# A fused transformer kernel: the chosen experts' rows gathered token by token, against both expert tables read once in blocks and multiplied densely

## What is computed

```python
q = (hf @ wq).reshape(T, 8, 2, 128)
sc = einsum('thpd,pnd->thpn', q, subkeys)          # 2 x 128 scores for each head
top_v, top_i = top_k(sc, 16)
cand_v = top_v[:, :, 0, :, None] + top_v[:, :, 1, None, :]
cand_id = top_i[:, :, 0, :, None] * 128 + top_i[:, :, 1, None, :]
best_v, best_j = top_k(cand_v.reshape(T, 8, -1), 16)
ids = take_along_axis(cand_id, best_j); gates = softmax(best_v)
a = einsum('td,ted->te', x, take(u_tab, ids))      # 128 chosen experts for each token
w = gates * gelu(a)
y = einsum('te,ted->td', w, take(v_tab, ids))
```

## Time and profile before

| | |
|---|---|
| time, median of 3 runs | 1234.37 us (1232.9 to 1235.4) |
| profiled execution, first to last instruction | 1229.3 us |
| mean granted clock of TensorE | 0.907 of full speed |
| busy: TensorE products / VectorE / ScalarE / GpSimd | 82% / 52% / 22% / 43% of the span |
| read from HBM | 360.08 MB, 294 GB/s over the span |

### The profile page before, as it was taken

How to read it: one execution, slowest core, us unless ns; L and a number is a source line. 1 busy time by engine, 2 the same in 40 slices (tenths; PEclk the granted TensorE clock), 3 DMA queues, 4 the chain that set the end, 5 groups by cost and what they waited for, 6 DMA issues and landing times.

```text
span 1229.3 us, 11227 instructions
## 1 busy us (share of the span) xinstructions
PE 1009.4 (82%) x3303; PEld 544.6 (44%) x3303; DVE 638.0 (52%) x1482; ACT 274.1 (22%) x741; POOL 534.5 (43%) x589
## 2 busy tenths in 40 slices
PE   4999999799888519767867857777579999999998
PEld 4768557554443204323323323323224645566454
DVE  6447676684754339636737646664443324311532
ACT  4022322112211102111105111110111253313540
POOL 1300003566666757667657667575766001200100
PEclk9999999899989859979779868887778999999999
DMA  9997765899999989989999989898989736333300
GB/s 346 308 371 253 277 212 163 318 366 336 356 365 362 413 340 357 373 334 400 347 353 398 350 347 408 325 413 335 412 342 364 269 137 206 95 111 137 137 1 34
DMA packets 123697, 361.75 MB, mean 294 GB/s; under 512 B 13464, under 2 KB 20256, under 8 KB 123520
## 3 DMA queue, kind: packets, MB, share of 16 engines
q0 software_dynamic: 76000, 276.39, 59.3%
q1 hardware_dynamic: 45008, 82.97, 19.1%
q10 hardware_dynamic: 2640, 1.81, 0.5%
HBM read 360.08 MB, written 1.05 MB: 294 GB/s over the span
## 4 chain that ended last, share of the span: by engine, by line
PE 74%; issue 14%; DVE 5%; another core or an unknown queue 3%; DMA 2%; ACT 2%; POOL 0%; DVEq 0%; POOLq 0%; ACTq 0%
PE bank L1492 36%; PE bank L1536 13%; PE bank L1256 9%; PE bank L1305 2%; PE bank L1246 2%; PE bank L1237 2%; DVE R L1784 1%; PE bank L1574 1%; PE bank L1346 1%; DMA small<-in_c 1%; PE bank L1322 1%; PE bank L1438 1%; PE bank L1417 1%; PE bank L1269 1%
## 5 line engine op out<-in xcount | busy, mean ns | idle before, releaser
L1492 PE MATMUL bank<-wring,R 128*128 128x512 f32 x496 | 238.9, 628 | 54.6 <-issue 53.0
L2040 DVE CUSTOM_DVE_ANT_0 wring<-wring,bank 128x1024 f32<-128x1024 f32 x160 | 194.2, 1218 | 150.2 <-DMA wring<-in_peer_u,ids 108.7
L769 POOL DMA_INDIRECT wring<-in_peer_v,ids x160 | 152.2, 951 | 125.4 <-issue 61.2
L1492 PEld LDWEIGHTS bank<-wring,R 128*128 128x128 f32 x496 | 98.2, 200 | 191.4 <-issue 186.8
L769 POOL DMA_INDIRECT wring<-in_peer_u,ids x160 | 152.9, 956 | 52.0 <-issue 44.2
L1536 PE MATMUL bank<-wring,hT 128*128 128x512 f32 (+1 forms) x384 | 167.4, 588 | 3.0 <-ACT R L1187 2.5
L1492 PE MATMUL bank<-R,modb 128*128 128x512 f32 x192 | 93.8, 635 | 58.3 <-ACT modb L998 38.2
L808 POOL TENSOR_SCALAR small<-small 128x2 f32<-128x2 f32 (+3 forms) x16 | 3.1, 194 | 304.4 <-ACTq L865 160.7
L1536 PEld LDWEIGHTS bank<-wring,hT 128*128 128x128 f32 x384 | 71.1, 190 | 83.8 <-issue 79.6
L1492 PE MATMUL bank<-hT,modb 128*128 128x512 f32 x96 | 63.2, 758 | 50.9 <-issue 49.1
L1492 PEld LDWEIGHTS bank<-R,modb 128*128 128x128 f32 x192 | 38.7, 203 | 111.6 <-issue 72.6
(11 more groups left out here) (292 smaller groups left out, 1326.4 us busy)
## 6 DMA issues: line engine op xcount, KB each, us to landing
wring<-in_w_in SPq DMA_DIRECT2D x12, 2048.0 KB, 12.1
wring<-in_ada_w SPq DMA_DIRECT2D x8, 2048.0 KB, 13.5
wring<-in_w_out SPq DMA_DIRECT2D x6, 2048.0 KB, 10.4
wring<-in_ada_w SPq DMA_DIRECT2D x8, 1024.0 KB, 14.7
wring<-in_peer_wq SPq DMA_DIRECT2D x2, 2048.0 KB, 7.9
wring<-in_w_in SPq DMA_DIRECT2D x4, 1024.0 KB, 10.6
wring<-in_w_in SPq DMA_DIRECT2D x2, 1792.0 KB, 12.6
wring<-in_peer_u,ids POOLq DMA_INDIRECT x160
```

Source lines behind the costliest of these rows:

```text
L769: pool.indirect_dma_start(dst, None, table, bass.IndirectOffsetOnAxis(index, 0)).then_inc(landed, 16)
L1492: last = pe.matmul(pb[half][:, :], diag[b][:, s, :], v_place(n, b, s)[:, half * 512:(half + 1) * 512], start=False, stop=closing and s == ...
L2040: dve.tensor_tensor_reduce(row, row, h_psum(t), 1.0, 0.0, ALU.mult, ALU.add, a8[:, b, s:s + 1]).then_inc(u_free, 1)
```

## The change

The gathers go away. SP reads U in 128 blocks of 128 experts (0.5 MB each, in order), TensorE transposes each block (8 transposes) and multiplies it with all 256 tokens (8 products of 256 columns), and ScalarE stores the Gelu of all 16384 x 256 activations in `experts`, which covers `wring` and `R` together. VectorE chooses for all heads in one go, and softmax is taken once. Then each token gets a dense 128x128 map of its gates: VectorE writes for every token two one-hot matrices of 128x128 (`left` and `right`, one of them scaled by the gates; `sides`), TensorE multiplies them (`gate_maps`, four tokens in a bank), and VectorE multiplies the map into `experts` for the blocks that are done (`j` of them), while ScalarE copies the rest of the map to where later blocks will stand; such a later block is parked and multiplied in when it is there. At last V is read in 128 blocks and multiplied densely, in both tiles for 112 blocks, then 16 blocks for tile 0 and the same 16 backwards for tile 1 (10 of them are read again). The queries and the scores stand in TensorE's sequence before and between the first blocks. Core of the diff:

```diff
+BLOCKS = 128
+GATES_FROM = 48
+U_PLACES = 3
+PARKED = 5
+V_PLACES = 6
+TAIL = 16
+TOKENS = 4
+BATCHES = NT * P // TOKENS
+def expert_schedule():
+    router = [("pq", 0, 0), ("pq", 0, 1), ("T", 0), ("sc", 0, 0), ("sc", 1, 0)]
+    rest = []
+    for ch in range(1, 4):
+        rest += [("pq", ch, 0), ("pq", ch, 1), ("sc", 0, ch), ("sc", 1, ch)]
+    out = list(router)
+    for j in range(BLOCKS):
+        if j + 1 < BLOCKS:
+            out.append(("T", j + 1))
+        out.append(("act", j))
+        if j < len(rest):
+            out.append(rest[j])
+        if j == GATES_FROM - 6:
+            out.append(("exp",))
+        if j == GATES_FROM - 3:
+            out += [("sel", t) for t in range(NT)]
+        done = sum(job[0] == "G" for job in out)
+        if j >= GATES_FROM:
+            out += [("G", b) for b in range(done, min(done + 1 + j % 2, BATCHES))]
+    return out
...
+def value_uses():
+    both = [(j, t, j) for j in range(BLOCKS - TAIL) for t in range(NT)]
+    first = [(j, 0, j) for j in range(BLOCKS - TAIL, BLOCKS)]
+    second = [(BLOCKS - 1 - m, 1, BLOCKS - 1 - m if m < V_PLACES else BLOCKS + m - V_PLACES) for m in range(TAIL)]
+    return both + first + second
...
+        experts = store[:, :].rearrange("p (j t) -> p j t", t=S)
+        u_rows = [modb[:, i, :] for i in range(U_PLACES)]
+        uT = [hrow[:, i, :].rearrange("p (k n) -> p k n", k=KD) for i in range(2)]
...
             await_full(sp, ("ada", 11))
             sp.wait_ge(rows_ready, 4 * NT)
-            sp.dma_start(fourth_queries, chunk_dram(peer_wq, 0, 1536, 2048)).then_inc(queries_landed[3], 16)
+            for j in range(BLOCKS):
+                if j >= U_PLACES:
+                    await_full(sp, ("T", j - U_PLACES, 1))
+                sp.dma_start(u_rows[j % U_PLACES], peer_u[0, j * P:(j + 1) * P, :]).then_inc(u_landed[j % U_PLACES], 16)
...
-            sp.wait_ge(u_free, NG * GROUP)
+            for n, (j, place) in enumerate(value_loads()):
+                if n == 0:
+                    await_full(sp, ("G", BATCHES - 1))
+                elif n == 2:
+                    await_full(sp, ("T", BLOCKS - 1, 1))
+                elif n == 5:
+                    sp.wait_ge(merged, len(merge_of))
+                elif n >= V_PLACES:
+                    sp.wait_ge(v_free, n - V_PLACES + 1)
+                sp.dma_start(v_rows[place], peer_v[0, j * P:(j + 1) * P, :]).then_inc(v_landed[place], 16)
...
+                elif job[0] == "T":
+                    j = job[1]
+                    if j >= 2:
+                        await_full(act, ("act", j - 2))
+                    for g in range(2):
+                        pb = await_full(act, ("T", j, g))
+                        free(act.activation(uT[j % 2][:, 4 * g:4 * g + 4, :], quad(pb[:, :]), ACT.Copy), ("T", j, g))
+                elif job[0] == "act":
...
+                elif job[0] == "exp":
+                    act.wait_ge(softmax_shift, 1)
+                    act.activation(chosen[:, :, 2, :], chosen[:, :, 2, :], ACT.Exp).then_inc(gate_exp, 1)
...
+            def transpose_experts(j):
+                pe.wait_ge(u_landed[j % U_PLACES], 16 * (j // U_PLACES + 1))
+                for g in range(2):
+                    pb = claim(pe, ("T", j, g))
+                    for i in range(4):
+                        a = (4 * g + i) * P
+                        last = pe.transpose(pb[:, i * P:(i + 1) * P], u_rows[j % U_PLACES][:, a:a + P], ident)
+                    full(last, ("T", j, g))
+
+            def activations(j):
+                for g in range(2):
+                    drained(pe, ("T", j, g))
+                pb = claim(pe, ("act", j))
+                for k in range(KD):
+                    last = pe.matmul(pb[:, 0:S], uT[j % 2][:, k, :], hT[:, k, :], start=k == 0, stop=k == KD - 1)
+                full(last, ("act", j))
+            def gate_maps(b):
+                pe.wait_ge(sides_ready, b + 1)
+                pb = claim(pe, ("G", b))
+                for i in range(TOKENS):
+                    last = pe.matmul(pb[:, i * P:(i + 1) * P], left[b % 2][:, i, :], right[b % 2][:, i, :], start=True, stop=True)
+                full(last, ("G", b))
...
+            for n, (j, t, load) in enumerate(uses):
+                place = loads[load][1]
...
                 for half in range(2):
+                    last = pe.matmul(pb[:, :], experts[:, j, t * P:(t + 1) * P], v_rows[place][:, half * 512:(half + 1) * 512], start=first, stop=final)
...
+            transpose_tile("zT", 0, 4 * NT, 0)
...
+            def sides(b):
+                for i in range(TOKENS):
+                    dve.tensor_scalar(left[b % 2][:, i, :], iota, chosenT[:, t, 0, c + i:c + i + 1], None, ALU.is_equal)
+                for i in range(TOKENS):
+                    ins = dve.tensor_scalar(right[b % 2][:, i, :], iota, chosenT[:, t, 1, c + i:c + i + 1],
+                                            chosenT[:, t, 2, c + i:c + i + 1], ALU.is_equal, ALU.mult)
+                ins.then_inc(sides_ready, 1)
+            for job in expert_schedule():
+                if job[0] == "G":
...
+                    w = experts[:, 0:j, b * TOKENS:(b + 1) * TOKENS]
+                    free(dve.tensor_tensor(w, quad(pb[:, :]).rearrange("p t n -> p n t")[:, 0:j, :], w, ALU.mult), job)
+                    if b + 2 < BATCHES:
+                        sides(b + 2)
```

More of the change, by code:

```diff
@@ L184, in y_schedule, with before, value_loads @@
     return out
[L187 to L195, removed]
+def expert_schedule():
[18 more added lines that the diff above has]
+    return out
+def before(job, kind):
+    order = expert_schedule()
+    return sum(e[0] == kind for e in order[:order.index(job)])
+def value_uses():
[3 more added lines that the diff above has]
+    return both + first + second
+def value_loads():
+    loads = [(j, j % V_PLACES) for j in range(BLOCKS)]
+    loads += [(BLOCKS - 1 - V_PLACES - m, (BLOCKS - 1 - m) % V_PLACES) for m in range(TAIL - V_PLACES)]
+    return loads
 def mla_schedule():
@@ L437, in program @@
[L437 to L458, removed]
@@ L968, in _ @@
             evac_oT(1)
[L969 to L974, removed]
             for t in range(NT):
@@ new lines, in transpose_choice @@
+            def transpose_choice(t):
+                if t == 0:
+                    pe.wait_ge(chosen_ready, 1)
+                pb = claim(pe, ("sel", t))
+                for i in range(3):
+                    last = pe.transpose(pb[:, i * P:(i + 1) * P], chosen[:, t, i, :], ident)
+                full(last, ("sel", t))
+            def gate_maps(b):
[4 more added lines that the diff above has]
+                full(last, ("G", b))
@@ new lines, in _ @@
+            drained(pe, ("G", BATCHES - 1))
+            loads = value_loads()
+            uses = value_uses()
+            for n, (j, t, load) in enumerate(uses):
+                place = loads[load][1]
+                if all(u[2] != load for u in uses[:n]):
+                    pe.wait_ge(v_landed[place], 16 * sum(e[1] == place for e in loads[:load + 1]))
+                if t == 0 and j in merge_of:
+                    pe.wait_ge(merged, merge_of[j] + 1)
+                first = all(u[1] != t for u in uses[:n])
+                final = all(u[1] != t for u in uses[n + 1:])
+                for half in range(2):
+                    pb = claim(pe, ("peer", t, half)) if first else bank[banks.jobs[("peer", t, half)][0]]
+                    last = pe.matmul(pb[:, :], experts[:, j, t * P:(t + 1) * P], v_rows[place][:, half * 512:(half + 1) * 512], start=first, stop=final)
+                    if final:
+                        full(last, ("peer", t, half))
+                if not final and all(u[2] != load for u in uses[n + 1:]):
+                    last.then_inc(v_free, 1)
@@ L1903, in _, with add_gated @@
             scale_heads(1)
-            def add_gated(job, gate, ch, t, ready=None):
+            def add_gated(job, gate, ch, t, ready=None, ytmp=ytmp):
                 pb = await_full(dve, job)
@@ new lines, in _, with choose @@
+            pairs = [(cand[:, h, :], best_v[:, h, :], best_j[:, h, :]) for h in range(2)]
+            def choose(t, g):
+                drained(dve, ("sc", t, g))
+                k, here = 4 * t + g, slice(g * 2 * TOPK, (g + 1) * 2 * TOPK)
+                halves = [(scores[:, k, j, :], top_v[:, j // 2, j % 2, :], top_i[:, j // 2, j % 2, :]) for j in range(4)]
+                for units in (halves, pairs):
+                    if units is pairs:
+                        chain.link(dve.tensor_tensor(cand.rearrange("p h (a b) -> p h a b", a=TOPK),
+                                                     bc(top_v[:, :, 0, :].unsqueeze(3), 2, TOPK, TOPK),
+                                                     bc(top_v[:, :, 1, :].unsqueeze(2), 2, TOPK, TOPK), ALU.add))
@@ L2011, in _ @@
[L2011 to L2020 removed]
+                    chain.wait()
```

(23 more changed lines are left out.)

543 lines of the change are left out of this document (127 added, 416 removed).

## The result

The changed kernel takes 1591.34 us (median of 4 runs, 1590.89 to 1591.83), the one before 1234.05 us in the same session: 1.291 times as long, interval 1.287 to 1.295. The forecast was 1610 us, 1588 to 1700, slower. A second session gave 1591.78 and 1233.14 us, 1.290 (1.287 to 1.293).

What follows compares the result with a forecast made beforehand. The gathers were taken to bound the experts' part (757 us); TensorE's sum replaces them: 203.7 + 1111.8 + 17 + 3 = 1335.5 us, then 268.6, 1 and 5.1 us, about 1610 us, range 1588 to 1700.

Steps and rivals of the forecast that it cites:

- Queries and scores: TensorE's query products (55.3 us) and score products (7.1 us), most of which had been hidden under the gathers.
- Transposes: TensorE transposing U, 128 blocks of eight at 0.107 us each: 110.1 us.
- Changes from one kind of work to the next: About 330 switches between kinds of TensorE work at 0.05 us each: 17 us, bounds 0 and 50 us.
- Waits in the first groups: TensorE waiting for ScalarE's copies in the first groups of the experts' part: 3 us.
- Behind the experts: Everything after the products with V: 268.6 us as before, plus 1 us for tile-0 transposes and copies moved there.
- From span to time: Difference between the profile's span and the median time: 5.1 us, taking 1605 to 1610 us.
- What had to stay hidden: Loads of U and V, ScalarE's copies, VectorE's choice and gate maps were to fit under TensorE's work in the experts' part.
- Waits in the long sequence (1): TensorE waits on VectorE's maps or in unexplained gaps in the experts' part: some 1675 us, 1640 to 1720; 19%.
- The clock (2): Transposes hold TensorE at 1.2 GHz in the stage with U: +442 us, about 2050 us; 6%.
- That the reading sets the pace (3): Dense products run as fast as tables arrive, so the experts' part lasts 380 us: 857 us in all; 3%.
- the condition that I gave for it: Reading decides once a pair of blocks, one of U and one of V, costs TensorE under 4.98 us; forecast 7.75.
- Overlap of products in long rows (4): Products overlap better in long rows than the profile rows show; at a tenth less, 1500 us; 2%.

Runs made afterwards that it cites:

- e4: Changed kernel with four more reductions of 128x384 on VectorE for each map, results unread: 1613.75 us, 22.4 more.
- e3: Changed kernel with each transpose of U done three times into the same place: 1814.5 us, 223.2 more.
- e1: Changed kernel with 252 of the 512 products with V left out, all tables still read: 1396.1 us, 195 less.
- e5: Changed kernel with the products with U in bf16, ScalarE writing the bf16 operands: 1292.5 us, 1.042 against the kernel before.
- e6: Changed kernel with products with U, experts' weights and rows of V all in bf16: 1058.3 us, 0.854 against the kernel before.
- e2: Kernel before with some 250 of 504 products with V rows left out, all gathers kept: 1149.95 us against 1151.22 us on that chip.

## Why the prediction was right

The mechanism was TensorE's sum in place of the gathers, and it held by its terms:

- *Start, 203.7 us*: 203.29.
- *Queries and scores, 62.4 us*: some 3 us more, since the first 32 products took 16.91 us, not 13.8. The sum took the full clock for all products, and these did not have it. In the new order both tiles' tokens are transposed ahead of any query, so TensorE stood idle for 5.75 us before the last transposes, where it had tile 0's products (L1417) before, and the granted clock was 0.50 until 207 us (the level of 1.2 GHz) and 1.00 from 212 us on. Half of 4 us and a fifth of 5 us are the 3 us:

```profile
200.33 1.97 PE L1155 MATMUL bank<-const,hrow 128*128 128x128 f32 x8 [5.75 <-DVE hrow L1831]
```

```profile
203.00:207.00 4.00, 3.71 (x9) 3.02 (x10) 0.00 (x0) 0.00 (x0) 2.16 (x4) 0.50 1.01 389
207.00:212.00 5.00, 5.00 (x20) 4.21 (x19) 0.00 (x0) 0.00 (x0) 0.00 (x0) 0.79 0.82 113
212.00:220.00 8.00, 8.00 (x39) 7.01 (x38) 0.00 (x0) 0.60 (x1) 0.00 (x0) 1.00 0.01 2
```

- *Transposes, 110.1 us*: 0.87 us for eight, 111.4. *Products with U, 442.2*: 128 x 3.46 = 442.9. *Maps, 57.1*: 0.89 for four, 57.0. *Products with V, 439.4*: 439.47. The prices of products came from stretches of the earlier trace rows where TensorE had waited for nothing. That of the transposes was read from a row of weight loads (`PEld`) in the earlier trace rows, and is right by luck: TensorE's own row there is 1.09 us, behind a wait, and in sequence it is 0.87.
- *Changes from one kind of work to the next, 17 us*: this is the term that was mis-sized. The chain shows no gap; the whole part is 1320.35 - 203.29 = 1117.1 us against 1111.8 computed without it. The first queries explain 3 of the difference of 5, and prices that were a little low the other 2. The 0.08 us in the earlier trace rows stood between such a weight load and a product, not between two products, so it was no price of a change. The chain of the kernel before has no gap at that place:

```profile
972.55 1.09 PE bank L1225 x8
973.64 3.12 PE bank L1536 x8
```

- *Waits in the first groups, 3 us*: not seen, the chain goes from work to work there.
- *Behind the experts, 269.6 us*: 268.85.
- *From span to time, 5.1 us*: 2.1 (1591.34 against 1589.2), mis-sized too. Every run on record lies 1.8 to 2.3 us above the span of its own execution, so the rest of the 5.1 was the spread between executions.

Together 15 + 1 + 3 us: the 19 us between 1610 and 1591. The 15 are the 20 us for changes and first waits and 0.4 of the start, less the 5 that the products took more. The mechanism held, but 1591 lies only 3 us above the lower end of the range, since both terms added for caution measured nothing; and that the sum without them, 1590, is so near is partly luck, since 5 us too little for the products stood against 4 us too much at the start, behind the experts and from span to time.

*What had to stay hidden* did. U landed in 3.6 us (median of its issues), where three places leave it over 8 us. The choice was done at 346.7 us, forecast 364, with 111 us of cover before `exp` at 458. VectorE's maps had 2 us of cover in each block (e4), by one-hot matrices that follow each other at 0.20 and 0.26 us.

*The rivals.* Waits in the long sequence (1) did not come: the gaps of the earlier trace rows are absent where DMA is at 0.3; whether the gathers' full queues caused them there was not tried. The clock (2) is refuted by e3 for up to 43% of transposes. That the reading sets the pace (3) is refuted by e1, and the condition that I gave for it is borne out from both sides. In e5 a pair of blocks costs TensorE 1.74 + 3.43 = 5.17 us, just above 4.98, and the kernel is slower than before by 4%. In e6 it costs 0.87 + 0.87 us for U and 0.86 us for V (an estimate, a fourth of 3.43), far below 4.98, and the kernel is faster than before. Overlap of products in long rows (4) is refuted by the 439.47 us.

## What to carry to other kernels

A gather that reads twice the bytes can still be the cheaper way in f32, when its dense replacement hands the work to an engine that takes four times as long for f32: count the new engine's work as products times the pace of a row without waits, and compare it with the time of the old stage (here 1112 against 757 us). Halving the traffic pays only as far as the next engine has room; here it paid (0.854) once the products with both tables were in bf16, and not yet with those of U alone (1.042). A busy share of 68 to 76% said nothing of TensorE's room; 432 us of real products in 757 us did, and e2 confirmed it: without half of them the time changed by 0.1%.

## What the runs showed of the hardware that I had not expected

The same kernel, bound by gathers, took 1151 us on one chip and 1233 to 1238 us on others. The gathers moved 412 GB/s there (in e2, its cut form) against 366 to 370, while the products with V took the same 439.47 us on each chip. So the ratio of these two kernels would be about 1591 / 1151 = 1.38 on that chip: an estimate, since it mixes sessions. Whether the chip itself or other use of its memory at the time sets the pace is not shown. The 366 to 370 GB/s are not a ceiling for all loads: in e6 plain loads of V moved 392 GB/s in a session in which the kernel before took 1238 us. Rows of products of different kinds and shapes, with transposes between, follow each other on TensorE with no gap over 0.02 us for over 1100 us. And a wait of 5.75 us ahead of a row of products cost more than itself: the granted clock was 0.50 behind it, and 32 products took 3 us longer.
